# A two-layer attention and mLSTM model on one core: attention output, gates and mixer 1 laid out by channel

## The chip, the core and the metric

The kernel runs on one core of a Trainium2 chip. TensorE (PE), VectorE (DVE), ScalarE (ACT), GpSimd (POOL) and SyncE (SP) each work through their own instructions in order and wait for one another by semaphores. The metric is device time in microseconds, lower is better. "PEld" is TensorE's loading of stationary weights, which overlaps its matmuls.

## The reference, cut to what matters

The input has 2048 latent tokens and 256 context tokens, each 1024 wide, in float32. Layer 1 is a mixer of attention and Fourier mixing, layer 2 a bidirectional mLSTM. Only layer 1 is touched. Its core is:

```python
def attend(q, k, v):                     # 12 query heads, 4 key/value heads, 64 wide
    s = jnp.einsum('bqhgd,bkhd->bhgqk', q, k) * (HEAD_DIM ** -0.5)
    p = jax.nn.softmax(s, axis=-1)
    return jnp.einsum('bhgqk,bkhd->bqhgd', p, v)

def even_mixer(h_lat, h_ctx, w_in, ...):
    q, ga, k, v, u, gb = jnp.split(h @ w_in, EVEN_SPLITS, axis=-1)   # 768,768,256,256,256,256
    ...                                  # norms, rotation of q and k
    y = jnp.concatenate([a * jax.nn.silu(ga), f * jax.nn.silu(gb)], axis=-1)
    return y @ w_out
x = layer_norm(ALPHA * x + g_l * y_lat) * post_ln_gain + post_ln_bias
```

The latent queries attend to all 2304 tokens, the context queries to the 256 of the context. `f` is the Fourier mixing of `u`. "Gates" below means `silu(ga)` and `silu(gb)`, 1024 channels together.

## The kernel before, in words

The program is a chain of stages with a barrier after each: modulation, first projection (`projections`, `pj_`), key heads and context attention (`heads`, `hd_`, with `ContextAttention`, `ca_`), latent attention (`attention`, `al_`), Fourier mixing (`fourier`, `fo_`), mixer 1 (`mixer_out`, `mo_`), second projection (`p_`, `pa_`, `pb_`), the mLSTM scan (`ml_`) and mixer 2 (again `mo_`).

**First projection.** 90 steps: five chunks of 512 columns (`c`), and in each chunk 18 tiles of 128 tokens (`t`). A step is 24 matmuls, in which 128 tokens are the stationary side and 512 weight columns move; each fp32 operand is split in a high and a low part (`split_mm`, L243). ScalarE makes the high part of a tile (L723), VectorE the low part (L855), two steps ahead. Chunks 3 and 4 are the gates; ScalarE evicts them with Silu (L762), SyncE stores them into `s_proj0` (L651). Between the steps, one tile every three steps, the query heads (`QueryHeads`) are loaded back, squared, rotated, transposed and stored. Every engine takes these parts at fixed steps of the same list.

**Latent attention.** 48 blocks of 512 queries of one head, two blocks (p = 0 and 1) to a loop turn. For each block TensorE computes scores twice. The first time (L2346), for the next block, is in 20 tiles with queries on partitions, of which VectorE takes the row maxima (L2269); they rotate over three PSUM slots, so tile x waits for the maximum of tile x - 3. VectorE joins the maxima and negates them (L2275), and SyncE moves them by DMA into the extra row of `qb` (L2158). The second time (L2358, L2359) the keys are on partitions and the row is included, so ScalarE can take the exponential straight away (L2209). The values (L2368) then add up in one PSUM bank: even key tiles in partitions 0 to 63, odd ones in 64 to 127. GpSimd and VectorE add up the exponentials for the denominators (L2235 to L2246, L2283, L2286) into `asum`. ScalarE copies the accumulator to `ot` (L2216), and `folded` (L2380, L2381) adds its two halves with an identity matrix as the moving side and sums `asum` over partitions with a column of ones. The result has tokens on partitions; VectorE takes 4 reciprocals per partition (L2290) and multiplies (L2294), SyncE stores it in `s_attn`, a row per token.

In TensorE's order a block is: values 6 to 8 of the block before, two maxima tiles, scores 0, two maxima tiles, scores 1, and so on, with three values groups in front of scores 3 and 6; `folded` stands between scores 7 and 8.

**Context attention** does the same in small in the heads stage: products with a column of ones beside the values (L1807), a reciprocal of 2 elements per partition (L1812).

**Fourier mixing** ends with 18 result tiles, copied out of PSUM by VectorE (L2587) and stored to `s_four`; the mixer's weights are loaded, split and prepared beside it (L2448, L2452, L2456).

**Mixer 1.** 18 tiles of 128 tokens. Loads of attention, Fourier and gate rows (L2710 to L2712), product (L2839), eight transposes on TensorE (L2884), high part (L2747), low part (L2843), 48 matmuls, then residual, layer norm, gain and store. Transposes of tile n + 1 stand in front of the matmuls of tile n.

## Time and profile before

| what | us |
|---|---|
| median of three runs | 3727.72 (3726.23 to 3730.48) |
| the profiled execution | 3721.77 |
| its span | 3720.1 |
| TensorE matmuls busy | 3435.6 (92%) |
| VectorE busy | 2290.1 (62%) |
| GpSimd busy | 1843.1 (50%) |
| ScalarE busy | 1334.7 (36%) |

Busy time is what an engine's instructions cover; the rest is waiting. The latent attention takes 732 to 1864 us of the span, mixer 1 about 1945 to 2186.

### The profile page before, as it was taken

To read this page: it belongs to the slowest core of one execution; us is meant where nothing else is said; L and a number is where in the kernel's file an instruction comes from. 1 tells how busy PE (TensorE), PEld (TensorE's weight loads), DVE (VectorE), ACT (ScalarE), POOL (GpSimd) and SP (SyncE) were. 2 spreads that over 40 slices of the span, in tenths; PEclk is the share of its full clock that TensorE was granted. 3 is DMA by queue.
4 is the path that set the end of the run, shared out by engine and by line. 5 is a ranking of instruction groups with operands and counts; after the bars stand their busy time and mean duration, and the time that the engine had idled before them with its cause. 6 is when DMAs were issued, how large, how long until landed. Compare 5 with 4: busy or idle time off the path is not lost. (4 is left out here: it accounts for less than half of the span.)

```text
span 3720.1 us, 51212 instructions
## 1 busy us (share of the span) xinstructions
PE 3435.6 (92%) x16884; PEld 2586.8 (70%) x16884; DVE 2290.1 (62%) x3492; ACT 1334.7 (36%) x2240; POOL 1843.1 (50%) x1294
## 2 busy tenths in 40 slices
PE   6999997799999999999959979989999998999798
PEld 4787884456666666666558869877778786887586
DVE  4666642766666666666536654366575645777576
ACT  2432333434444444444320123333443422664200
POOL 1133413657777777777723333433586612444364
PEclk7999997799999999999979989999999999999899
DMA  5234535511111111111065545655545446677563
GB/s 189 99 106 133 142 105 179 189 28 35 34 35 34 37 35 38 35 37 34 17 206 172 189 133 171 206 189 158 175 129 173 142 150 206 214 221 241 198 217 133
DMA packets 357715, 480.18 MB, mean 129 GB/s; under 512 B 83308, under 2 KB 209276, under 8 KB 357392
## 3 DMA queue, kind: packets, MB, share of 16 engines
q1 hardware_dynamic: 291744, 342.18, 29.9%
q10 hardware_dynamic: 54256, 97.73, 8.8%
q0 software_dynamic: 11520, 37.77, 2.6%
q8 instruction: 109, 1.79, 0.2%
q14 instruction: 86, 0.70, 0.1%
HBM read 339.75 MB, written 137.72 MB: 128 GB/s over the span
## 5 line engine op out<-in xcount | busy, mean ns | idle before, releaser
L2269 DVE TENSOR_REDUCE al_mx<-al_sx 128x1 f32<-128x512 f32 (+1 forms) x960 | 562.7, 632 | 267.3 <-PE al_sx L2346 253.7
L2209 ACT ACTIVATE al_e<-al_st 128x1024 f32<-128x1024 f32 x432 | 443.0, 1026 | 579.4 <-PE al_st L2359 569.2
L2239 POOL TENSOR_TENSOR al_acc_p<-al_acc_p,al_e 128x1024 f32<-128x1024 f32 x192 | 456.7, 2379 | 19.8
L245 PE MATMUL pb_acc<-p_whi,pb_r_hi 128*128 128x512 f32 x952 | 378.6, 398 | 39.0 <-DVE pb_r_lo L1616 28.3
L2368 PE MATMUL al_acc<-al_e,vres 128*64 128x512 f32 x1728 | 402.5, 601 | 0.0
L247 PE MATMUL pb_acc<-p_whi,pb_r_lo 128*128 128x512 f32 x952 | 376.3, 395 | 0.0
L246 PE MATMUL pb_acc<-p_wlo,pb_r_hi 128*128 128x512 f32 x952 | 375.5, 394 | 0.0
L1616 DVE TENSOR_TENSOR pb_r_lo<-pb_stg,pb_r_hi 128x512 fp32r<-128x512 f32 x238 | 248.6, 1047 | 165.8 <-ACT pb_r_hi L1514 161.6
L2358 PE MATMUL al_st<-al_qa,kres 128*128 128x512 f32 x864 | 344.7, 399 | 3.6 <-DMA al_qb<-al_negm 3.2
L2359 PE MATMUL al_st<-al_qb,kres 128*128 128x512 f32 x864 | 340.3, 394 | 0.0
L2235 POOL TENSOR_TENSOR al_acc_p<-al_e 128x1024 f32<-128x1024 f32 x48 | 160.3, 3340 | 306.3 <-ACT al_e L2209 306.3
L2346 PE MATMUL al_sx<-kres,al_qx 128*128 128x512 f32 (+1 forms) x960 | 298.1, 393 | 13.3 <-DMA al_qx<-s_q 11.0
L245 PE MATMUL pj_acc<-pj_whi,pj_h_hi 128*128 128x512 f32 x720 | 285.3, 396 | 0.0
L2346 PEld LDWEIGHTS al_sx<-kres,al_qx 128*128 128x128 f32 x960 | 171.9, 191 | 162.2 <-issue 125.8
L247 PE MATMUL pj_acc<-pj_whi,pj_h_lo 128*128 128x512 f32 x720 | 281.8, 391 | 0.0
L246 PE MATMUL pj_acc<-pj_wlo,pj_h_hi 128*128 128x512 f32 x720 | 281.7, 391 | 0.0
L855 DVE TENSOR_TENSOR pj_h_lo<-pj_hall,pj_h_hi 128x1024 fp32r<-128x1024 f32 x90 | 131.0, 1457 | 207.1 <-ACT pj_h_hi L723 207.1
L2368 PEld LDWEIGHTS al_acc<-al_e,vres 128*64 128x64 f32 x1728 | 111.2, 136 | 211.2 <-issue 194.8
L1514 ACT ACTIVATE pb_r_hi<-pb_stg 128x512 fp32r<-128x512 f32 x238 | 149.2, 628 | 270.0 <-PE pb_acc L247 252.6
L245 PEld LDWEIGHTS pb_acc<-p_whi,pb_r_hi 128*128 128x128 f32 x952 | 181.6, 191 | 84.1 <-DVE pb_r_lo L1616 34.2
L245 PE MATMUL mo_acc<-ow_whi,mo_y_hi 128*128 128x512 f32 x544 | 215.6, 396 | 0.0
L247 PE MATMUL mo_acc<-ow_whi,mo_y_lo 128*128 128x512 f32 x544 | 212.8, 391 | 0.0
(320 smaller groups left out, 7287.3 us busy)
## 6 DMA issues: line engine op xcount, KB each, us to landing
pb_stg<-s_hsum ACTq DMA_DIRECT2D x238, 256.0 KB, 2.7
s_proj<-pj_stage SPq DMA_DIRECT2D x90, 256.0 KB, 2.1
s_proj<-pb_out SPq DMA_DIRECT2D x72, 256.0 KB, 3.0
p_wst<-in_w1s ACTq DMA_DIRECT2D x18, 1024.0 KB, 5.9
ml_k<-s_proj SPq DMA_DIRECT2D x36, 512.0 KB, 4.3
ml_v<-s_proj SPq DMA_DIRECT2D x36, 512.0 KB, 8.8
mo_in<-s_proj SPq DMA_DIRECT2D x34, 512.0 KB, 6.3
hm_w<-in_ada_w SPq DMA_DIRECT2D x16, 1024.0 KB, 9.8
```

The source lines that it names most:

```text
L245: nc.tensor.matmul(out, s_hi, m_hi, start=start, stop=False)
L246: nc.tensor.matmul(out, s_hi, m_lo, start=False, stop=False)
L247: return nc.tensor.matmul(out, s_lo, m_hi, start=False, stop=stop)
L1616: V.tensor_tensor(r_lo[:, g % RING], stg[:, g % NSTG], r_hi[:, g % RING].bitcast(F32), ALU.subtract).then_inc(lo_done, 1)
L2209: nc.scalar.activation(e[:, pair(p, j), :, :], st[(NP * p + j) % 2][:, :, 0:W], ACT.Exp).then_inc(e_done, 1)
L2235: nc.gpsimd.tensor_tensor(acc_p[:], e[:, pair(p, 2)], e[:, pair(p, 5)], ALU.add).then_inc(add_p, 1)
L2239: nc.gpsimd.tensor_tensor(acc_p[:], acc_p[:], e[:, pair(p, j)], ALU.add).then_inc(add_p, 1)
L2269: V.tensor_reduce(mx[:, x:x + 1], slots[x % NSX][:, 0:spans[x % NS][1]], AX.X, ALU.max).then_inc(sx_max, 1)
L2346: mm(slots[x % NSX][:, 0:width], qx[:, p, i * P:(i + 1) * P], kres[:, g, lo:lo + width], start=True, stop=True).then_inc(sx_mm, 1)
L2358: mm(dst[:, t, 0:W], kres[:, g, keys], qa[:, p, :], start=True, stop=False)
L2359: y = mm(dst[:, t, 0:W], kres[:, NKV + g, keys], qb[:, p, :], start=False, stop=True)
L2368: y = mm(acc[t * HD:(t + 1) * HD, 0:W], vres[:, 2 * j + t, g, :], e[:, pair(p, j), t, :], start=(j == 0), stop=(j == NP - 1))
```

## The change

**Attention by channel.** The two halves of the accumulator are no longer folded by TensorE. ScalarE copies one half (64 partitions), and VectorE adds the other from PSUM (`joined`): the even block's result goes to `even`, which ScalarE copies to the lower half of `un`, the odd block's to the upper half. TensorE's next values wait for this sum (`un_done`) instead of for ScalarE's copy. Denominators are made for two blocks at once: a 128 x 64 matrix of ones is stationary, `asum` moves, so that the sum stands on 64 partitions. ScalarE copies it out of PSUM, VectorE takes the reciprocal in four pieces of 128 columns between the maxima of the odd block, and one product gives both blocks. The result is stored by channel.

```diff
+            def joined(n, p, v):
+                half, other = slice(p * HD, (p + 1) * HD), slice((1 - p) * HD, (2 - p) * HD)
+                dve.wait_ge(ot_done, n + 1)
+                if p == 0 and not (fixed(n) and n < 2):
+                    dve.wait_ge(kept, v)
+                V.tensor_tensor(even[:] if p == 0 else un[half, :], acc[other, 0:W], ot[half, :], ALU.add).then_inc(un_done, 1)
+            def inverse(v, i):
+                dve.wait_ge(den_out, v + 1)
+                V.reciprocal(rden[:, piece(i)], den[:, piece(i)]).then_inc(rden_done, 1)
+            def norm(v):
...
+                V.tensor_tensor(o[:], un[:], rden[:], ALU.mult).then_inc(o_done, 1)
...
             def body(g, n, p, v, nxt):
+                if started and p == 1:
+                    joined(n - 1, 0, v)
+                elif started:
+                    joined(n - 1, 1, v - 1)
...
                     if j == 7 and nxt is not None:
                         bias(n + 1, 1 - p, v + p)
-                    if j == 8 and started:
-                        norm(n - 1, 1 - p, v - 1 + p)
+                    if paired and j in (1, 2, 4, 5):
+                        inverse(v - 1, (1, 2, 4, 5).index(j))
+                    if paired and j == 7:
+                        norm(v - 1)
```

On TensorE and ScalarE:

```diff
-            def folded(n, p):
...
-                for i in range(nq):
-                    at, cols = i * (HD + 1), slice(i * P, (i + 1) * P)
-                    mm(fo[:, at:at + HD], ot[:, p % 2, cols], fold[:, 0:HD], start=True, stop=True)
-                    y = mm(fo[:, at + HD:at + HD + 1], asum[:, p % 2, cols], ones[:], start=True, stop=True)
-                y.then_inc(fold_mm, 1)
+            def denominators(n, v):
+                pe.wait_ge(asum_done, n + 2)
...
+                for i in range(2):
+                    y = mm(fo[i * HD:(i + 1) * HD, 0:W], ones[:], asum[:, i, :], start=True, stop=True)
+                y.then_inc(den_mm, 1)
...
-                    if j == 7 and started:
-                        folded(n - 1, 1 - p)
+                    if j == 7 and p == 0 and started:
+                        denominators(n - 2, v - 1)
...
+                nc.scalar.activation(ot[half, :], acc[half, 0:W], ACT.Copy).then_inc(ot_done, 1)
+                nc.scalar.activation(den[:], fo[:, 0:W], ACT.Copy).then_inc(den_out, 1)
+                nc.scalar.activation(un[0:HD, :], even[:], ACT.Copy).then_inc(kept, 1)
```

The context attention does likewise: 64 values columns, then 64 columns of ones, stationary; a reciprocal of 256 columns for every two heads.

**Gates by channel.** In chunks 3 and 4 the weights are stationary and up to four token tiles (512 tokens) move. A group of four tiles is four steps: the first two do the first half of the 1024 inputs, the last two the second half, so the four results of a group appear in its last two steps; five PSUM banks rotate. The result goes to a new `s_gt`, a row per channel. The query heads load into two buffers instead of three.

```diff
+    turned_q = [c >= GATED if L0 else C1_Q <= c * CH < C1_Q + D for c, _ in steps]
+    base = [k - t % 4 if turned_q[k] else k for k, (_, t) in enumerate(steps)]
...
+    ahead = [min(K - 1, base[k] + (5 if tiles[k] == 4 and k > base[k] else 3) if turned_q[k] else k + (1 if c == 0 else 2)) for k, (c, _) in enumerate(steps)]
...
+            def turned_products(k, c):
...
+                if n == 4:
+                    pe.wait_ge(lo_done, first + (2 if step < 2 else 4))
+                    half, columns = step // 2, range(step % 2 * 2, step % 2 * 2 + 2)
+                    part = range(half * KP, half * KP + KP)
...
+                        mm = split_mm(nc, dst, whi[:, c % 2, i, at:at + P], wlo[:, c % 2, i, at:at + P], moving(h_hi, k, i), moving(h_lo, k, i), i == 0, i == KD - 1)
```

**Fourier and mixer 1.** The last Fourier matmuls swap their sides, and their result stays in SBUF (`four`) by channel: no `s_four`, no stores. Mixer 1 loads attention and gates by channel (rows of 128 tokens, 512 B) and does the product in two parts, straight in the layout that the matmuls need; its transposes go, and the product of tile n + 2 moves in front of the normalisation. Loads of a tile now wait for the low part two tiles before.

```diff
-                    sp.dma_start(ins[:, p, 0, 0:QW], s["attn"][rows, :]).then_inc(in_ld[p], 16)
-                    sp.dma_start(ins[:, p, 0, QW:D], s["four"][rows, :]).then_inc(in_ld[p], 16)
-                    sp.dma_start(ins[:, p, 1, :], s["proj0"][rows, C_GATE:W0_COLS]).then_inc(in_ld[p], 16)
+                    sp.dma_start(ins[:, p, 0, 0:QW].rearrange("p (k n) -> p k n", n=P), s["attn"][:, rows].rearrange("(k p) n -> p k n", p=P)).then_inc(in_ld[p], 16)
+                    sp.dma_start(ins[:, p, 1, :].rearrange("p (k n) -> p k n", n=P), s["gt"][:, rows].rearrange("(k p) n -> p k n", p=P)).then_inc(in_ld[p], 16)
...
             def turned(n, p, v):
+                if L0:
+                    return
```

## Rows read from the trace of the kernel before

**Rows 1.** Busy time by stretch: start:end, length, then PE, PEld, DVE, ACT, POOL, clock.
```profile
400.00:603.00 203.00, 201.30 (x912) 166.57 (x910) 89.76 (x81) 69.76 (x89) 43.99 (x23) 1.00 0.38 107
603.00:732.00 129.00, 82.02 (x424) 43.81 (x424) 78.32 (x209) 64.48 (x351) 93.79 (x125) 0.72 0.76 241
732.00:1864.00 1132.00, 1116.52 (x5184) 684.22 (x5184) 757.17 (x1200) 471.82 (x480) 792.52 (x336) 0.99 0.13 34
1945.00:2186.00 241.00, 216.34 (x1016) 180.45 (x1014) 154.33 (x196) 26.95 (x31) 82.27 (x76) 0.95 0.49 170
```

**Rows 2.** Timeline of TensorE, one attention block: start, duration, engine, line, tiles, count.
```profile
1000.65 2.80 PE L2368 MATMUL al_acc<-al_e,vres 128*64 128x512 f32 x12
1003.37 0.73 PE L2346 MATMUL al_sx<-kres,al_qx 128*128 128x512 f32 x2
1003.94 0.39 PE L2358 MATMUL al_st<-al_qa,kres 128*128 128x512 f32 x1
...
1004.87 0.62 PE L2346 MATMUL al_sx<-kres,al_qx 128*128 128x512 f32 x2
...
1020.88 0.33 PE L2380 MATMUL al_sx<-al_fold,al_ot 128*128 128x64 f32 x2
...
1022.58 0.49 PE L2358 MATMUL al_st<-al_qa,kres 128*128 128x512 f32 x1
...
1023.70 2.79 PE L2368 MATMUL al_acc<-al_e,vres 128*64 128x512 f32 x12
```

**Rows 3.** Timeline of VectorE in the same block; idle time before and its releaser in brackets.
```profile
1003.91 3.66 DVE L2269 TENSOR_REDUCE al_mx<-al_sx 128x1 f32<-128x512 f32 x6 [3.56 <-PE al_sx L2346]
...
1009.32 2.33 DVE L2283 TENSOR_TENSOR al_acc_d<-al_e 128x1024 f32<-128x1024 f32 x1
...
1016.20 1.22 DVE L2286 TENSOR_TENSOR al_acc_d<-al_acc_d,al_e 128x1024 f32<-128x1024 f32 x1
...
1021.10 0.17 DVE L2275 TENSOR_REDUCE al_negm<-al_mx 128x4 fp32r<-128x20 f32 x1
```

**Rows 4.** Timelines of ScalarE and GpSimd in the same block.
```profile
1003.49 0.60 ACT L2216 ACTIVATE al_ot<-al_acc 128x512 f32<-128x512 f32 x1 [1.71 <-PE al_acc L2368]
...
1009.29 1.27 POOL L2246 TENSOR_TENSOR al_asum<-al_acc_p 128x512 f32<-128x512 f32 x1
1016.25 3.41 POOL L2235 TENSOR_TENSOR al_acc_p<-al_e 128x1024 f32<-128x1024 f32 x1 [5.68 <-ACT al_e L2209]
```

**Rows 5.** VectorE's groups by form: count, then busy us, mean ns of one.
```profile
L1635 DVE TENSOR_TENSOR pb_out<-pb_acc,pb_s 128x512 f32<-128x512 f32 x34 | 23.4, 689 | 36.5 <-PE pb_acc L247 36.5
L3087 DVE RECIPROCAL ml_den<-ml_den 128x1 f32<-128x1 f32 x128 | 21.0, 164 | 4.4
L2290 DVE RECIPROCAL al_rden<-al_sx 128x4 f32<-128x4 f32 x48 | 8.8, 183 | 85.8 <-PE al_sx L2381 85.8
```

**Rows 6.** Negated maxima (durations, first and last start) and the first scores.
```profile
L2275 DVE TENSOR_REDUCE al_negm<-al_mx x48: 173/174/175, 744.5 to 1826.2; 128x4 fp32r<-128x20 f32 x48
...
748.70 0.77 PE L2358 MATMUL al_st<-al_qa,kres 128*128 128x512 f32 x1 [3.24 <-DMA al_qb<-al_negm]
```

**Rows 7.** Timeline of mixer 1: its start, and one tile change.
```profile
1937.89 1.23 DVE L2839 TENSOR_TENSOR mo_y<-mo_in 128x1024 f32<-128x1024 f32 x1 [12.03 <-DMA mo_in<-s_proj]
...
1946.27 0.78 PE L245 MATMUL mo_acc<-ow_whi,mo_y_hi 128*128 128x512 f32 x1
...
2005.18 1.03 PE L2884 MATMUL mo_tp<-keep_ident,mo_y 128*128 128x128 f32 x8
...
2005.97 0.48 PE L245 MATMUL mo_acc<-ow_whi,mo_y_hi 128*128 128x512 f32 x1
```

**Rows 8.** DMA issues: count, KB each, median us from issue to landing.
```profile
ml_qt<-s_qt SPq DMA_DIRECT2D x32, 512.0 KB, 6.2
```

**Rows 9.** Timeline at the end of the Fourier stage.
```profile
1929.42 2.34 POOL L2456 TENSOR_TENSOR ow_wlo<-ow_wst,ow_whi 128x1024 fp32r<-128x1024 f32 x1 [1.38 <-ACT ow_whi L2452]
```

**Rows 10.** Waits, 180 to 603 us: total us, times, longest.
```profile
ACT hq_hi L306 <- DMA s_q<-hq_lo: 145.5, 17, 14.5
```

More of the change, by code:

```diff
@@ L607, in projections, with source, slot, moving @@
     w1_st = hall[:, 0:KP, NT - 4:, :].rearrange("p k t n -> p k (t n)")
+    def source(k):
+        n, t = tiles[k], steps[base[k]][1]
+        part = slice((k - base[k]) * KD // n, (k - base[k] + 1) * KD // n)
+        return hall[:, part, t:t + n, :]
+    def slot(h, k):
+        return h[:, k % RING].rearrange("p (k t) n -> p k t n", t=tiles[k])
+    def moving(h, k, i):
+        per = KD // tiles[k]
+        return slot(h, base[k] + i // per)[:, i % per]
     def evicted(eng, k):
@@ L2180, in body @@
                     row(n + 1, 1 - p)
-                if not (fixed(n) and n == 0):
-                    store(n - 1, prev_p(p, 1))
+                if p == 1 and not (fixed(n) and n < 2):
+                    store(n - 3, v - 1)
                 if more:
@@ L2188, in _ @@
             over_blocks(sp, body)
[L2189 to L2191 removed]
+            store(TOTAL - 2, TOTAL // 2 - 1)
+            sp.wait_ge(stored, 16 * TOTAL)
         @block.scalar
@@ L2330, in _ @@
             over_blocks(dve, body)
-            norm(TOTAL - 1, TOTAL - 1, (TOTAL - 1) // 2)
+            joined(TOTAL - 1, 1, TOTAL // 2 - 1)
+            for i in range(NPIECE):
+                inverse(TOTAL // 2 - 1, i)
+            norm(TOTAL // 2 - 1)
         @block.tensor
@@ L2498, in _ @@
                 out_weights.load(sp, k)
[L2499 to L2508 removed]
+            for k in range(2, KD):
+                out_weights.load(sp, k)
         @block.gpsimd
```

334 lines of the change are left out of this document (181 added, 153 removed).

## The prediction

> **What bounds the kernel now.** I read the stages first. TensorE's matmul side is busy 1116.5 of 1132.0 us in the latent attention, 216.3 of 241.0 in mixer 1 and 201.3 of 203.0 in the gate chunks of the first projection; only the heads stage leaves it idle (82.0 of 129.0) [rows 1]. So in three of the four stages that the change touches, an instruction taken from TensorE is worth its time, unless its gap is filled by a wait. Then the timeline of one attention block, because 48 of them make the stage. The stretch from 1000.65 to 1023.70, values to values, is one block: 23.05 us [rows 2]. In it VectorE has 0.36 to 3.6 us of idle time in four places, about 6.6 us in all [rows 3]: it is not the bound, but it stands one step behind TensorE, since a score tile for the maxima may be overwritten only when the maximum three before it is done.
>
> **Attention, what goes.** Per block, eight fold and eight denominator matmuls: first at 1020.88, next scores at 1022.58, 1.70 us, and those scores start 0.33 us apart in place of 0.23, so 1.80 us [rows 2]. What comes: per two blocks two fp32 matmuls of 64 columns by 512, four passes. The values have that form: twelve passes from 1000.65 to 1003.37, 0.227 each [rows 2], so 0.91 and about 0.2 for the switches: 1.1 us. The other bounds for it are nothing and the fold's own 1.8. If nothing else were late, a pair of blocks went from 46.10 to 46.10 - 3.60 + 1.10 = 43.60 us: 2.5 us for each of 24 pairs, 60 us. That is the most that this part can give.
>
> **What is late next.** Three new things sit on VectorE, which must feed the maxima.
> 1. The joined sum (accumulator half plus ScalarE's copy) is the first instruction of a block in VectorE's order. It waits for ScalarE's copy, 0.60 us from 1003.49 [rows 4], and costs 0.69 like the 512-column operations from PSUM [rows 5]. Counted from the block's start (1000.65): copy 2.84 to 3.44, joined 3.48, first maximum 4.08 in place of 3.26 [rows 3]. Its result is there at 4.81; TensorE wants the slot for the fourth score tile at 4.45 (the pair at 1004.87 [rows 2], second 0.23 later). A slip of 0.36 us in every block. What queues behind joined is all of VectorE's block; who waits is TensorE. Values of the next block need the accumulator at 7.4, joined is done at 4.2: no loss there. ScalarE's two extra copies per pair (0.6 us each) run while TensorE does values, where ScalarE idles 1.71 us before its copy [rows 4].
> 2. The reciprocal now has 128 columns in each of four pieces. The trace has it with 1 and 4 elements: 164 and 183 ns [rows 5], so 6.3 ns an element and 183 + 124 x 6.3 = 0.97 us a piece, 3.9 us a pair, all in the odd block. The low end is 0.18 (a fixed cost only), the high end 46 ns an element (183 by 4), which the 1-element row speaks against; I take 0.97, since only the two rows together say how it grows. In the odd block, after the fourth maximum, piece 0 runs 6.48 to 7.38, so the fifth maximum comes at 7.84 instead of before 7.45: slip 0.39. Piece 1 pushes the first addition from 8.67 to 10.6; there it no longer meets GpSimd's sum and takes 1.2 instead of 2.3 us [rows 3, 4], which gives 1.1 back. Piece 2 delays the thirteenth maximum to 15.51, wanted at 15.17: slip 0.34. Piece 3 puts the second addition at 17.8 (it was at 15.55), in the middle of a GpSimd addition; I let it wait to 18.55, which costs 0.15 more at the last score tile. Sum of slips in the odd block: 0.36 + 0.39 + 0.34 + 0.15 = 1.24.
> 3. The row of negated maxima goes by DMA to the next block's first scores. At the start of the stage that path stands free: negation at 744.5, scores at 748.70, waiting for the DMA: 4.2 us [rows 6]. In steady state they are 5.9 us apart (1021.10 to 1003.94 + 23.05 = 1026.99), so 1.7 us of slack and the fold is 1.8 of it. In the odd block the row lands 0.25 us late; in the even block the 1.1 us of denominators cover it.
>
> Even block: 23.05 - 1.80 + 1.10 + 0.36 = 22.7; odd: 23.05 - 1.80 + 1.24 + 0.25 = 22.7. Pair 45.4 against 46.1: 0.7 x 24 = 17 us gained of the possible 60. The end of the stage has no cover: denominators, ScalarE's copy, four reciprocals, product and store stand in a row. Fold, reciprocal and product took about 4.2 us after the last sum; now 1.7 (matmuls at the low clock) + 0.65 + 3.9 + 0.7 = 7.0: **+2.7 us**. Bounds of the whole attention part: -57 (all hidden) to +40 (third rival).
>
> The Trainium skill, VectorE: DVE Perf Modes, "First, the fixed hardware budget", says that Reciprocal is an iterative divide with a repeat count of 8. At the page's 0.96 GHz this would be 8.3 ns an element, an estimate of 1.2 us a piece, where the two rows say 6.3 ns. By the page the odd block would lose some 0.6 us more, attention gain only 3 us, and the total come out near 3715.
>
> **Heads stage.** Context attention: reciprocal of 256 columns per two heads, 183 + 252 x 6.3 = 1.77 us, six times, for twelve of 2 elements (under 0.18, by the rows of 1 and 4 [rows 5]); products and matmuls come out even. +8.6 us of VectorE work in a stage where it is busy 78.3 of 129.0 [rows 1]; the last pair stands at the end of the stage and costs 1.6 us openly. Bounds 1.6 and 8.6; I take **+3**.
>
> **Gate chunks.** Weights stand and 512 tokens move: 24 matmuls of 512 columns a step as before, the same conversions and the same 256 KB stores. Nothing to gain where TensorE is busy 99% [rows 1]. But results of a group of four steps come only in its last two, so ScalarE, which evicts in order, stands up to 2.5 steps behind, and with it SyncE's stores and the query heads' loads and stores queued behind them on SyncE. ScalarE already waits 8.6 us on average for the store of the query heads, 17 times [rows 10], and TensorE hides it with five steps of lead. One case of scaled queries behind two conversions held until the middle of the third step costs half a step (2.7 us), three more about 0.5: **+4**, bounds 0 and +25 (half a step in each of nine groups).
>
> **Fourier mixing.** The same matmuls with operands swapped, the same evictions into SBUF. The eighteen stores go and the weights' loads move past them on SyncE, but the stage ends with GpSimd's low part of the last weights at 1929.42 + 2.34 = 1931.76 [rows 9]; that chain (load, ScalarE, GpSimd, two buffers) is untouched. **0**; up to 2 us of gain.
>
> **Mixer 1.** Eight transposes per tile: 2005.18 to 2005.97 and 0.1 us for the slower start after them, 0.89 us [rows 7], for 17 tiles in the steady part: **-15**. The period falls from 11.5 to 10.6 us. VectorE does 8.6 us a tile there (154.3 by 18 [rows 1]), so it doesn't take over. The start: gate product at 1937.89, first product of the mixer at 1946.27, with two transposed tiles and conversions between [rows 7]. Now product 1.4, high part 1.0, low part 1.2: 1941.6. The load in front may be slower for its shorter rows; I allow 0.7: **-4**. The loads get rows of 512 B: the queries of the scan, 512 KB in such rows, land in 6.2 us [rows 8]. Attention and gates together are 896 KB: 10.8 us if all of the 6.2 grows with the bytes, 6.2 if none does; I take 9, since small transfers have a fixed part too. They may start when the low part two tiles earlier is done, one period (10.6 us) before they are wanted, so they fit, narrowly.
>
> **Sum.** -17 + 2.7 + 3 + 4 + 0 - 15 - 4 = -26 us. The profiled execution took 3721.8 us (span 3720.1), 6 us under the median of 3727.7; durations hardly differ, so I take the difference off the median: 3701.
>
> **Rivals.**
> - All of VectorE's work finds room (shorter reciprocals, or maxima with more slack than I read): attention gains 57. For it: 6.6 us of idle in each block [rows 3] against 2.4 us of added work a block (2 x 0.69 + 3.9 + 0.69 less two old reciprocals and products, about 1.2, by 2). Against: the idle stands after TensorE's values, not where the pieces are. 3727.7 - 57 + 3 + 4 - 19 = 3659.
> - The gates' and attention's loads bind mixer 1, and its 15 us are lost: 3716. For it the 6.2 us row; against it a DMA share of 0.49 in the stage [rows 1].
> - The gate chunks starve TensorE for half a step per group, +25 instead of +4: 3722.
> - The other side: VectorE becomes the bound in the odd blocks through the port that it shares with GpSimd. An addition that starts beside one of GpSimd's takes 2.33 us instead of 1.22, as at 1009.32 against 1016.20, and at 1016.25 it is GpSimd that waits (3.41 instead of 2.4) [rows 3, 4]. Pieces move the second addition behind GpSimd's first; if GpSimd's chain, 2.4 us each with 0.1 between, keeps the port for one more, the maxima and the negation come 2.4 us later and TensorE waits for all of it: odd block 25.1, pair 47.8, 24 x 1.7 = +41 in place of -17: 3760. It decides from a wait above 0.7 us + what the sum has (pair above 46.1). The Trainium skill, SBUF - State Buffer, "SBUF: two separate sides", calls this port pair an exclusive lock held for the whole instruction by whichever starts first, for VectorE operations with two SBUF inputs; the trace agrees with it (2.33 against 1.22), and by it only the additions and the last product can be hit, not maxima, reciprocals or joined sums.
>
> **Chances.** My forecast 0.50; all hidden 0.22; loads bind mixer 1 0.08; gate chunks 0.07; port 0.13. A measurement of this kernel can tell 0.2%, 7.5 us, from no change. Faster: the first three, 0.80; same: the fourth, 0.07; slower: 0.13. Own range of the forecast 3685 to 3718; the range for 8 in 10 reaches to the hidden case and past the fourth: 3655 to 3735.
>
> **What would show it.** Attention period of 45.4 us a pair; reciprocals of about 0.97 us; TensorE waiting at the fourth score tile for VectorE's maximum, 0.3 to 0.4 us a block; even blocks without a wait for the row, odd ones with a short one. Mixer 1 with a period near 10.6 us and its first product about 4 us earlier after the stage's start. Gate chunks with TensorE idle of a few us. It would be wrong if the pair were at 43.6 (then the slips are none) or over 46.1, or if the second additions took over 2.4 us, or if mixer 1 waited for its loads.

## The result, and the profile after

The changed kernel takes 3763.9 us (median of 4 runs, 3760.6 to 3768.1), the kernel before 3727.0 in the same comparison. The ratio is 1.0105, 95% interval 1.0091 to 1.0119: slower by 39 us (37 between the two medians) where 26 us less were forecast. The profiled execution took 3761.6 us, its span is 3759.9. The stages from both traces, by the starts of the instructions named (us). One trace has a scatter of its own: in the eleven traces with the changed kernel's gate chunks these take 217.9 to 222.1 us, and in the ten with its heads stage that takes 147.7 to 153.6.

| from ... to | before | after | change | forecast |
|---|---|---|---|---|
| start to the projection's last product | 600.9 | 622.8 | +21.9 | +4 |
| to the first latent score tile (heads stage) | 131.6 | 150.8 | +19.2 | +3 |
| to the last latent scores | 1115.8 | 1122.8 | +7.0 | -17 |
| to the Fourier stage's first load | 17.1 | 22.6 | +5.6 | +2.7 |
| to mixer 1's first product | 80.9 | 74.6 | -6.3 | -4 |
| to mixer 1's last product | 211.0 | 198.6 | -12.5 | -15 |
| to the end | 1562.8 | 1567.8 | +5.0 | 0 |

The busy time by stretch (start:end, length, then PE, PEld, DVE, ACT, POOL, granted clock, DMA share, GB/s) of the changed kernel: gate chunks, heads, latent attention, mixer 1's products. In the gate chunks TensorE was never idle between two products; now it is for 11.2 us, and for 0.5 more at the head of the stretch shown. The attention loses 18 us of TensorE's work and still gets longer.

```profile
404.00:623.00 219.00, 207.36 (x1008) 174.15 (x1008) 85.69 (x81) 67.23 (x86) 40.19 (x23) 0.98 0.34 97
623.00:773.00 150.00, 96.03 (x425) 45.13 (x424) 85.13 (x197) 65.20 (x352) 87.87 (x119) 0.77 0.66 207
773.00:1919.00 1146.00, 1098.86 (x4512) 591.68 (x4512) 868.81 (x1272) 496.55 (x528) 799.46 (x336) 0.98 0.13 33
1993.00:2192.00 199.00, 198.48 (x863) 164.10 (x864) 145.05 (x195) 19.88 (x18) 85.78 (x69) 0.98 0.57 188
```

**Gate chunks.** The timeline of the changed kernel around its longest gap, SyncE, ScalarE, VectorE, GpSimd, TensorE, and the busy time behind two gaps. SyncE stands for 7.42 us at the stores of results that are not finished (488.26); the query heads' stores queued behind them land late, so ScalarE can overwrite the high part only at 501.63. ScalarE itself stands for 4.59 us at such a result (494.73), so the weights' high part comes late, GpSimd's low part of it (497.27), and behind that the query heads' scale `hq_rs` (503.11). VectorE's conversions take 6.01 us beside GpSimd's (2.36 alone), then VectorE waits 1.28 us for that scale (506.34). The query heads' low part comes at 507.22, and TensorE, whose transposes need it, has waited 5.47 us. So the last waits of this gap end on GpSimd and VectorE, and not on ScalarE's high part.

```profile
488.26 7.42 SPq L674 DMA_DIRECT2D s_gt<-pj_stage  x2
...
494.73 0.60 ACT L788 ACTIVATE pj_stage<-pj_acc 128x512 f32<-128x512 f32 x1 [4.59 <-PE pj_acc L247]
...
501.63 0.81 ACT L310 ACTIVATE hq_hi<-pj_tp 128x768 fp32r<-128x768 f32 x1 [2.62 <-DMA s_q<-hq_lo]
...
498.11 6.01 DVE L881 TENSOR_TENSOR pj_h_lo<-pj_hall,pj_h_hi 128x1024 fp32r<-128x1024 f32 x2 [3.82 <-ACT pj_h_hi L749]
...
506.34 0.96 DVE L361 TENSOR_TENSOR hq_turn<-hq_turn,hq_rs 128x768 f32<-128x768 f32 x1 [1.28 <-POOL hq_rs L334]
507.22 0.95 DVE L367 TENSOR_TENSOR hq_lo<-pj_tp,hq_hi 128x768 fp32r<-128x768 f32 x1
...
497.27 4.62 POOL L823 TENSOR_TENSOR pj_wlo<-pj_wst,pj_whi 128x2048 fp32r<-128x2048 f32 x1 [9.85 <-ACT pj_whi L733]
...
503.11 3.13 POOL L334 TENSOR_TENSOR hq_rs<-hq_rs,hq_power 128x12 f32<-128x12 f32 x1
...
508.32 1.51 PE L375 MATMUL pj_tp<-keep_ident,hq_turn 128*128 128x128 f32 x6 [5.47 <-DVE hq_lo L367]
...
451.00:476.00 25.00, 24.79 (x115) 20.51 (x116) 10.23 (x12) 9.77 (x12) 9.32 (x5) 1.00 0.45 133
508.00:533.00 25.00, 24.68 (x154) 22.86 (x155) 13.01 (x13) 7.39 (x10) 8.21 (x5) 0.93 0.33 91
```

**Heads.** One pair of tiles of the changed kernel. The pairs repeat every 14.8 us (reciprocals at 690.33, 705.20, 720.02), where two tiles took about 10 before. TensorE waits 2.73 us for the turned keys and then runs its values at about half the rate (3.55 us for eight; 1.94 at the full clock). VectorE's 1.76 and 0.42 us stand between values and the next turned keys.

```profile
694.45 0.65 PE L2108 MATMUL hd_tk<-keep_ident,hd_rot 128*128 128x128 f32 x4 [2.73 <-DVE hd_rot L2060]
...
695.51 3.55 PE L1855 MATMUL ca_res<-ca_e,ca_v 128*64 128x256 f32 x8
...
703.22 1.94 PE L1855 MATMUL ca_res<-ca_e,ca_v 128*64 128x256 f32 x8
...
705.20 1.76 DVE L1863 RECIPROCAL ca_rden<-ca_res 128x256 f32<-128x256 f32 x1 [0.72 <-PE ca_res L1855]
706.99 0.42 DVE L1865 TENSOR_TENSOR ca_o<-ca_res,ca_rden 128x256 f32<-128x256 f32 x1
...
708.58 0.69 DVE L2060 TENSOR_TENSOR hd_rot<-hd_turn,hd_rs 128x512 f32<-128x512 f32 x1
```

**Latent attention.** The 48 negations give the period: first and last start, 47 blocks apart, so the mean pair is (1876.1 - 785.5) / 23.5 = 46.41 us; before it was 46.03 [rows 6]. "Mean pair" below is always that.

```profile
L2349 DVE TENSOR_REDUCE al_negm<-al_mx x48: 173/174/176, 785.5 to 1876.1; 128x4 fp32r<-128x20 f32 x48
```

TensorE, ScalarE, VectorE and GpSimd in the even block from 1019.29 to 1042.81 and, for the second addition, in the odd one behind it. The fourth score tile starts at 1024.57, 0.71 us after the third where it was 0.23 [rows 2]. The first addition (1029.00) waits 0.18 us for GpSimd's combining sum, then takes 2.32 us beside GpSimd's last sum. The product takes 2.61 us beside GpSimd's chain, and 2.6 or more in 16 of the 24 of the run (0.69 in the others). ScalarE's copy of the even result waits 1.32 us for it (1021.82), and the accumulator's copy stands behind (1022.48). In the odd block the second addition takes 2.10 us beside GpSimd's first sum (22 of the 24 take over 2 us), where it took 1.22 before [rows 3]. The reciprocal shown is of the odd block before.

```profile
1024.57 0.50 PE L2435 MATMUL al_sx<-kres,al_qx 128*128 128x512 f32 x1 [0.32 <-DVE al_mx L2343]
...
1040.66 1.08 PE L2467 MATMUL al_sx<-al_asum,al_ones 128*64 128x512 f32 x4
...
1021.82 0.63 ACT L2284 ACTIVATE al_un<-al_even 64x512 f32<-64x512 f32 x1 [1.32 <-DVE al_o L2382]
1022.48 0.59 ACT L2270 ACTIVATE al_ot<-al_acc 64x512 f32<-64x512 f32 x1
...
1003.11 0.94 DVE L2373 RECIPROCAL al_rden<-al_den 128x128 f32<-128x128 f32 x1
...
1019.12 2.61 DVE L2382 TENSOR_TENSOR al_o<-al_un,al_rden 128x512 f32<-128x512 f32 x1 [0.22 <-issue]
1023.11 0.68 DVE L2368 TENSOR_TENSOR al_un<-al_acc,al_ot 64x512 f32<-64x512 f32 x1 [1.38 <-ACT al_ot L2270]
...
1029.00 2.32 DVE L2357 TENSOR_TENSOR al_acc_d<-al_e 128x1024 f32<-128x1024 f32 x1 [0.18 <-POOL al_acc_p L2316]
...
1060.57 2.10 DVE L2360 TENSOR_TENSOR al_acc_d<-al_acc_d,al_e 128x1024 f32<-128x1024 f32 x1
...
1026.51 2.39 POOL L2316 TENSOR_TENSOR al_acc_p<-al_acc_p,al_acc_d 128x1024 f32<-128x1024 f32 x1
1028.98 1.27 POOL L2320 TENSOR_TENSOR al_asum<-al_acc_p 128x512 f32<-128x512 f32 x1
...
1059.23 2.36 POOL L2309 TENSOR_TENSOR al_acc_p<-al_e 128x1024 f32<-128x1024 f32 x1 [5.91 <-ACT al_e L2262]
```

**End of the attention.** The last values start at 1896.62 (1848.60 before); GpSimd's last sum ends 12.2 us later (9.9 before), and from there denominators, copy, four reciprocals, product and store take 10.1 us (6.8 before).

```profile
1907.54 1.26 POOL L2320 TENSOR_TENSOR al_asum<-al_acc_p 128x512 f32<-128x512 f32 x1
1908.86 1.97 PE L2467 MATMUL al_sx<-al_asum,al_ones 128*64 128x512 f32 x4 [9.44 <-POOL al_asum L2320]
1910.88 0.60 ACT L2277 ACTIVATE al_den<-al_sx 128x512 f32<-128x512 f32 x1 [10.82 <-PE al_sx L2467]
1911.51 3.39 DVE L2373 RECIPROCAL al_rden<-al_den 128x128 f32<-128x128 f32 x4 [10.74 <-ACT al_den L2277]
```

**Mixer 1** starts with the gate product at 1989.82 and the first product 3.7 us later, 8.4 before [rows 7].

```profile
1989.82 0.96 DVE L2916 TENSOR_TENSOR mo_in<-mo_in 128x768 f32<-128x768 f32 x1 [9.85 <-DMA mo_in<-s_gt]
...
1993.52 0.79 PE L245 MATMUL mo_acc<-ow_whi,mo_y_hi 128*128 128x512 f32 x1 [14.17 <-DVE mo_y_lo L2931]
```

### The profile page after: what moved, and what is told of

The parts are those of the page before. It is cut to its first block and busy times, and to the rows that moved or that the text cites. A ratio compares the mean times of both kernels' runs of the same rounds, so it can differ in the third digit from the quotient of the medians.

```text
span 3759.9 us, 49801 instructions
## 1 busy us (share of the span) xinstructions
PE 3423.0 (91%) x16164; PEld 2492.1 (66%) x16164; DVE 2411.2 (64%) x3570; ACT 1361.3 (36%) x2288; POOL 1849.0 (49%) x1288
## 5 line engine op out<-in xcount | busy, mean ns | idle before, releaser
L2343 DVE TENSOR_REDUCE al_mx<-al_sx 128x1 f32<-128x512 f32 (+1 forms) x960 | 549.0, 625 | 63.4 <-PE al_sx L2435 58.9
L2313 POOL TENSOR_TENSOR al_acc_p<-al_acc_p,al_e 128x1024 f32<-128x1024 f32 x192 | 484.9, 2526 | 20.0 <-POOL al_acc_p L2313 0.4
L2435 PE MATMUL al_sx<-kres,al_qx 128*128 128x512 f32 (+1 forms) x960 | 331.4, 408 | 35.0 <-DVE al_mx L2343 21.8
L2309 POOL TENSOR_TENSOR al_acc_p<-al_e 128x1024 f32<-128x1024 f32 x48 | 139.0, 2896 | 308.2 <-ACT al_e L2262 308.2
L245 PE MATMUL mo_acc<-ow_whi,mo_y_hi 128*128 128x512 f32 x544 | 215.1, 395 | 14.2 <-DVE mo_y_lo L2931 14.2
L246 PE MATMUL mo_acc<-ow_wlo,mo_y_hi 128*128 128x512 f32 x544 | 213.5, 393 | 0.0
L2447 PEld LDWEIGHTS al_st<-al_qa,kres 128*128 128x128 f32 x864 | 163.0, 189 | 70.1 <-issue 36.9
L247 PEld LDWEIGHTS pb_acc<-p_whi,pb_r_lo 128*128 128x128 f32 x952 | 181.4, 191 | 40.3
```

The costliest lines, as they stand in the source:

```text
L245: nc.tensor.matmul(out, s_hi, m_hi, start=start, stop=False)
L246: nc.tensor.matmul(out, s_hi, m_lo, start=False, stop=False)
L247: return nc.tensor.matmul(out, s_lo, m_hi, start=False, stop=stop)
L2313: nc.gpsimd.tensor_tensor(acc_p[:], acc_p[:], e[:, pair(p, j)], ALU.add).then_inc(add_p, 1)
L2343: V.tensor_reduce(mx[:, x:x + 1], slots[x % NSX][:, 0:spans[x % NS][1]], AX.X, ALU.max).then_inc(sx_max, 1)
L2435: mm(slots[x % NSX][:, 0:width], qx[:, p, i * P:(i + 1) * P], kres[:, g, lo:lo + width], start=True, stop=True).then_inc(sx_mm, 1)
```

## The experiments

Ratios are to the kernel before, on the same chip; the changed kernel has 1.0105. "Gates" is first gate product to last product of the projection, "heads" to the first latent score tile, "end" from the last latent scores to the Fourier stage's first load, all in us. e2, e4 and e7 leave work of the reference out; they only measure.

| run | ratio, 95% interval | what moved |
|---|---|---|
| e1 | 1.0068 (1.0051 to 1.0085) | gates 218.3 to 204.1 |
| e2 | 1.0050 (1.0033 to 1.0067) | heads 150.8 to 136.8 |
| e3 | 1.0118 (1.0101 to 1.0135) | mean pair 46.54 |
| e4 | 1.0078 (1.0061 to 1.0095) | mean pair 46.23, end 4.0 shorter |
| e5 | 1.0166 (1.0145 to 1.0188) | mean pair 47.2 |
| e6 | 1.0148 (1.0128 to 1.0168) | mean pair 47.0 |
| e7 | 1.0057 (1.0040 to 1.0073) | mean pair 45.76, end 5.2 shorter |
| e8 | 1.0092 (1.0064 to 1.0121) | heads 139.9 |
| e9 | 1.0092 (1.0075 to 1.0110) | mean pair 46.14 |
| e10 | 1.0023 (1.0013 to 1.0032) | gates 204.1, heads 136.7 |
| e11 | 1.0144 (1.0126 to 1.0163) | mean pair 46.88 |
| e12 (before) | 0.9995 (0.9982 to 1.0007) | mean pair 45.92 |
| e13 | 0.9996 (0.9987 to 1.0005) | mean pair 45.92 |
| e14 | 0.9995 (0.9986 to 1.0004) | mean pair 45.84 |
| e15 | 1.0097 (1.0082 to 1.0113) | mean pair 45.93 |
| e16 | 0.9967 (0.9954 to 0.9980) | mean pair 45.55 |
| e17 | **0.9923 (0.9909 to 0.9936)** | mean pair 44.78 |
| e18 (before) | 0.9994 (0.9984 to 1.0004) | mean pair 45.89 |

### e1: the order in the gate chunks

```diff
+    ended = [[base[k] + 2 * (k - base[k]) - 4 + i for i in range(2)] if tiles[k] == 4 and k > base[k] + 1
+             else [] if tiles[k] == 4 else [k] for k in range(K)]
-    ahead: base[k] + (5 if tiles[k] == 4 and k > base[k] else 3)
+    ahead: base[k] + (5 if tiles[k] == 4 and k > base[k] + 1 else 3)
 (scalar, sync, step k)
-    evict k; store k
+    for u in ended[k]: evict u; store u
```

> The changed kernel with another order in the gate chunks alone: ScalarE's evictions and SyncE's stores of a group of four steps stand in the order at the third and fourth step, where the results are finished, and the conversions for the next group one step later. No work is added or taken away. Theory: what the gate chunks lose (404.5 to 622.5 in the changed kernel, 218 us against 197) is TensorE waiting for the query heads' low part, which waits for ScalarE and SyncE standing behind evictions of unfinished results; 13.8 us of idle time and about 5 of the lower clock after it. Then the stretch falls to 199 to 205 us and the total to about 3747 (3743 to 3752). Rival: the form itself costs it (192 matmuls of 256 columns at 0.120 us instead of half of 0.221, banks, conversions for four tiles at once): the stretch stays above 212 and the total above 3757.

Gates 204.1 us, total -14: the theory holds. No gap is left in TensorE's row after the first product; one of 2.3 us is left ahead of it. The edit moves the evictions, the stores and two of the conversions together, so it shows that their order costs the 14 us, not how they share them.

```profile
406.00:610.00 204.00, 203.78 (x1005) 172.91 (x1006) 86.58 (x81) 66.84 (x85) 40.69 (x23) 0.99 0.37 105
```

### e2, e8, e10: the heads stage

```diff
 e2: -reciprocal(rden[:], res[:, W:2 * W])    +reciprocal(rden[:, 0:4], res[:, W:W + 4])
 e8: scaled(n); bias(n - 3)
+    norm(n - 7)
     normal(n); low_part(n - 1)
-    norm(n - 6)
 e10: e1 + e8, and on TensorE
-    scores(n - 5); values(n - 6); mod.products(n)
+    scores(n - 5); mod.products(n); values(n - 6)
```

> The changed kernel with the context attention's six reciprocals over 4 columns instead of 256 (the rest of the buffer holds ones, so the context's denominators are left out). Theory: the reciprocal stands on the path of each pair of tiles, transposes, values, reciprocal, product, turned keys, next transposes: 6 x 1.58 = 9.5 us of the stage's loss of 19.4 go (stage 150.6 to about 141), total 3754; the rest belongs to the values matmuls, 8 of 256 columns (1.94 us) where there were 8 of 65 (1.00). Rival 1: the reciprocal explains all of it, since its wait also drops the clock: stage 131 to 134, total 3745. Rival 2: it is hidden and the matmuls' form is all: stage 148 or more.

> The changed kernel with the context attention's reciprocal and product one tile later in VectorE's order, behind the next turned keys instead of ahead of them (and the store one tile later); nothing is left out. Theory: it is the order that puts 2.2 us between values and TensorE's next transposes, and TensorE's wait (2.73 us a pair) that drops its clock to 0.5 (3.55 us for eight values matmuls that take 1.94): the stage falls from 150.6 to 138 to 143, total about 3753. Rival: the values of the next even head wait for the product now, and the pair stays near 14.8 us: stage above 148, total above 3761.

> The changed kernel with the new order in the gate chunks (first experiment), the context's reciprocal and product one tile later (eighth), and the context's values on TensorE behind the modulation's products instead of ahead of them. Theory: the two stages' losses are independent and both are matters of order: gate chunks 204 us, heads stage at most 140 (lower if the values now find their denominators' product done, 132 to 138), total 3763 - 14 - 12 = 3737. Rival: what one stage gives comes back in the next (the heads stage was 2.8 us longer when the gate chunks were shorter): total above 3746.

e2 gives back 14.0 us (11 to 17 with the scatter of the stage), more than the 9.5 us of reciprocals in it: rival 1 was nearer, since the wait costs clock as well. TensorE's busy time for the same matmuls falls from 96.03 us (in 150) to 91.96. e8 leaves nothing out and gives 10.9; its total is unclear by itself (the interval reaches from -15 to +6 us against the changed kernel's 1.0105). e10 is clear: 31 us less than the changed kernel in all, heads 136.7. The reciprocal need not be shorter, it must not stand ahead of the next turned keys. The heads stages of e2, e8 and e10:

```profile
627.00:764.00 137.00, 91.96 (x429) 43.60 (x428) 76.04 (x198) 65.28 (x352) 89.64 (x119) 0.79 0.73 228
```

```profile
632.00:772.00 140.00, 92.83 (x426) 42.89 (x426) 87.07 (x197) 65.05 (x352) 90.21 (x119) 0.77 0.69 223
```

```profile
615.00:751.00 136.00, 91.80 (x424) 41.08 (x424) 87.04 (x197) 64.94 (x352) 89.92 (x119) 0.78 0.72 229
```

### e3 to e6: single moves on VectorE, and the reciprocals taken away

```diff
 e3: (vector, block) joined(n - 1) ahead of the first maximum -> behind the fourth
 e4: -V.reciprocal(rden[:, piece(i)], den[:, piece(i)])
     +V.reciprocal(rden[:, i * P:i * P + 4], den[:, i * P:i * P + 4])
 e5: add(n, p, 0) behind the eighth maximum -> behind the tenth
 e6: e3 + e5
```

> The changed kernel with the joined sum behind the fourth maximum of a block instead of ahead of the first, on VectorE alone. Theory: the joined sum at the head of the block makes TensorE wait at the fourth score tile, 0.58 and 0.60 us more than in the kernel before in the two blocks of a pair. With it behind, that wait is gone: pair of blocks 46.3 to about 45.2, attention 1145 to about 1118, total about 3737. Rival: VectorE is short of time in the whole first part of the block, and the wait only moves to the sixth or eighth tile: pair 46.0 or more, total above 3756.

> The changed kernel with each of the latent attention's four reciprocal pieces over 4 columns instead of 128 (the rest holds ones: most denominators are left out). Theory: 4 x 0.76 us go from VectorE in every second block, and with them the slips of 0.30 and 0.45 us at the eighth and the fourteenth to sixteenth score tile and about 0.15 elsewhere; the pair goes from 46.3 to 45.4, the end of the stage is 3.1 us shorter, total about 3739. Rival: the product beside GpSimd's additions (2.61 us where it takes 0.69 alone) is what delays the block, and the reciprocals are not: pair 46.1 or more, total above 3755.

> The changed kernel with VectorE's first addition of a block behind the tenth maximum instead of the eighth; nothing else. Theory (GpSimd's chain): that addition overwrites what GpSimd's combining sum reads, and runs beside GpSimd's last sum (2.33 us where it takes 1.22 alone); two maxima later GpSimd stands idle, 1.1 us of VectorE come back in each block that had it, and the slips at the tenth to sixteenth score tile (0.09 to 0.45 us) shrink: attention 1145 to about 1132, total about 3750. Rival: the addition filled the 2.7 us in which TensorE does values and VectorE has no tile; moved, it stands before tiles that are wanted, attention 1150 or more, total above 3765.

> The addition later as above, and the joined sum behind the fourth maximum. Theory (GpSimd's chain): with the joined sum late alone the slip at the fourth tile went (1.06 to 0.46 us) and came back at the tenth (0.58 to 1.00) and the eighth (0.84 to 1.61), where the addition waited 0.48 us for GpSimd's combining sum. With both moved no addition meets GpSimd: pair 46.3 to about 45.0, total about 3732. Rival (VectorE has no room at all): each shift only moves the slip, pair 46.2 or more, total above 3760.

All four theories fell; in e4 the rival did too by its total (3752, where it had over 3755). In e3 the fourth tile is on time (third and fourth tile 0.45 us together, 1.04 in the changed kernel), and the lost time comes back at the twelfth tile (its pair takes 1.00 for 0.58; the expectations call it the tenth) and the eighth (1.61 for 0.84): the first addition, now later, waits for GpSimd:

```profile
1033.84 2.33 DVE L2357 TENSOR_TENSOR al_acc_d<-al_e 128x1024 f32<-128x1024 f32 x1 [0.48 <-POOL al_acc_p L2316]
```

In e4 3.0 us of VectorE's work are gone from each pair, and the mean pair falls by 0.18 us only: the slips at the eighth and sixteenth tile are gone, but the first addition waits 1.11 us for the same sum, and the twelfth tile comes 0.94 later. So neither the joined sums nor the reciprocals are the loss by themselves. e5 takes the addition out of TensorE's values, where it stood free: its rival was right.

### e7, e9, e11, e12: GpSimd's chain and the fold

```diff
 e7: -tensor_tensor(acc_p[:], acc_p[:], e[:, pair(p, j)], ALU.add)
     +tensor_tensor(acc_p[:, 0, :], acc_p[:, 0, :], e[:, pair(p, j), 0, :], ALU.add)
 e9: (tensor, even block, ahead of values 0 to 2; ScalarE copies fo to un once a pair)
     +for i in range(2):
     +    mm(fo[i * HD:(i + 1) * HD, 0:W], fold[:], ot[:, i, :], start=True, stop=True)
     -V.tensor_tensor(even or un[half, :], acc[other, 0:W], ot[half, :], ALU.add)
 e11, e12: -IN_POOL = (2, 5, 4, 6, 7, 8)    +IN_POOL = (2, 4, 5, 6, 7, 8)
```

> The changed kernel with GpSimd's four chained additions over half of their columns (512 instead of 1024; half of these sums is left out, and the denominators get 1 added). Theory: the attention's period is a loop, late score tiles, late exponentials, GpSimd's chain (about 17 us of a block of 23.15) later by about 1 us than before the change, VectorE's first addition waiting for it, late maxima. With the chain 5 us shorter the addition waits for nothing: pair 46.3 to 45.0 or less, and the end of the stage 5 us shorter: total 3763 to about 3728. Rival: VectorE's own added work (joined sums, reciprocals, product) is the whole loss: pair 46.0 or more, only the end of the stage gains, total about 3756.

> The changed kernel with the two halves of the accumulator joined on TensorE again, once per pair of blocks, by channel (two matmuls of 64 columns by 512, as the denominators, ahead of the even block's first values; ScalarE copies both halves per block and the joined result once per pair). VectorE's two joined sums (0.69 us each) go. Theory: the joined sum is what makes the fourth score tile late; its slip of 0.6 us goes in both blocks, TensorE has 1.1 us more work a pair, and the first additions meet GpSimd's end as before: pair 46.3 to 45.9 to 46.2, total 3753 to 3762, with the fourth tile at 0.46 us in both blocks. Rival: the slip moves behind, as it did when the joined sum was only put later, and TensorE's 1.1 us come on top: pair above 47, total above 3785.

> The changed kernel with GpSimd's first sum of a latent block over the third and fifth exponentials instead of the third and sixth, so that its chain can start one step (1.4 us) earlier; the same five sums. Theory (GpSimd's chain sets when VectorE's first addition may run, and how late the end of the stage is): the chain ends 1.0 to 1.4 us earlier, the first addition takes 1.22 us instead of 2.33, attention falls by 10 to 24 us, total 3740 to 3753. Rival: the start now meets VectorE's second addition (1.22 us, 2.17 in one block of the pair already), which waits 2.4 us for it ahead of the last score tiles: pair above 46.5, total above 3768.

> The kernel before with the same earlier start of GpSimd's sums. If GpSimd's chain also sets the pace of the kernel before, it gains as the changed one does. Theory: there VectorE has room (6.6 us of idle a block), its additions' waits cost TensorE nothing, and only the end of the stage gets 1.4 us shorter: 3722 to 3727. Rival: it gains as much as the changed kernel, then the order is a reserve of both and no part of the explanation: below 3715.

e7 is the largest step of one edit to the changed kernel: 0.65 us a pair, though VectorE's work is all there. Both additions of the even block now take 1.2 us and most products 0.94. It is half of what the theory asked for. Its negations:

```profile
L2349 DVE TENSOR_REDUCE al_negm<-al_mx x48: 173/174/177, 788.6 to 1864.0; 128x4 fp32r<-128x20 f32 x48
```

e9: the fourth tile is on time in both blocks, as expected, and the pair pays about 1.0 us of TensorE for it. e11's rival was right: the second addition takes up to 3.37 us in odd blocks and 2.15 to 2.28 in even ones (mostly 2.18 and 1.22 in the changed kernel). e12: in the kernel before the second additions lengthen too (mostly 2.15 to 2.28 us, 1.22 without the edit), and its time stays the same.

### e13 to e18: place, and the combining sum

```diff
 e13: e10 + e9; (vector, odd block) pieces 0, 1 ahead of the first maximum, 2, 3 at j = 4, 5
 e14: as e13, but pieces 2, 3 and the product ahead of the next even block's first maximum
 e15, e16, e17, e18: the changed kernel, e13, e14, the kernel before, each with
      for i, j in enumerate(IN_POOL[2:]):
+         if i == 2:
+             gpsimd.tensor_tensor(acc_p[:], acc_p[:], acc_d[:], ALU.add).then_inc(comb_done, 1)
          gpsimd.tensor_tensor(acc_p[:], acc_p[:], e[:, pair(p, j)], ALU.add)
-     gpsimd.tensor_tensor(acc_p[:], acc_p[:], acc_d[:], ALU.add).then_inc(comb_done, 1)
```

> The tenth kernel (gate chunks and context in the new order) with the fold by channel of the ninth, and the first two reciprocals of a pair ahead of the odd block's first maximum instead of behind the fourth and the sixth. There VectorE is idle: negation at 1040.78, denominators copied at 1044.43, first maximum at about 1046 in the changed kernel. Theory (place, not sum): two of four reciprocals become free, the slip at the eighth tile (0.16 to 0.30 us) goes, the block reaches its first addition earlier: mean pair from 46.14 to 45.8 or less, total 3731.9 - 7 - 8 = 3717 (3712 to 3722). Rival (the sum counts, VectorE has no free time that TensorE does not pay): mean pair 46.1 or more, total 3724 or more.

> As the thirteenth, and the other two reciprocals and the product at the head of the next even block, ahead of its first maximum (3.3 us of idle time between the negation and the first score tile); the store follows there. Theory: the odd block loses all its slips from reciprocals (0.3 and 0.45 us), the even block pays up to 1 us where the product runs beside GpSimd's chain (1.1 to 2.6 us instead of 0.69): mean pair 45.4 to 45.7, total 3707 to 3715. Rival: the product, locked behind GpSimd's sums, makes the first four maxima late in every even block: mean pair above 46.2, total above 3727.

> The changed kernel with GpSimd's combining sum (of VectorE's part) ahead of its last two additions instead of behind them; the same work. VectorE's first addition of the next block then finds its buffer free some 5 us earlier. Theory (the semaphore): the addition goes between two of GpSimd's instructions and takes 1.2 us instead of 0.2 + 2.3, mean pair from 46.41 to 45.9 or less, total 3752 or less. Rival (the port): it waits as long for the instruction that GpSimd then has under way, mean pair 46.3 to 46.6, total 3759 to 3770.

> The thirteenth kernel with the combining sum sooner. Theory (the semaphore): mean pair from 45.92 to 45.4 or less, total 3709 or less against 3721 before. Rival (the port): 45.8 or more, total 3718 or more.

> The fourteenth kernel with the combining sum sooner. Its even blocks' first addition waited 2.38 us for the combining sum and then ran 2.33 beside GpSimd's last sum; the odd ones 0.67 and 2.32. Theory (the semaphore): mean pair from 45.84 to 45.0 or less, total 3700 or less. Rival (the port): 45.7 or more, total 3716 or more.

> The kernel before with the combining sum ahead of GpSimd's last two additions. Theory: there VectorE's wait behind GpSimd costs TensorE nothing (its score tiles start 0.44 to 0.57 us apart throughout), so the mean pair stays at 46.0 and the total within 5 us of 3721. Rival: it gains as e17 did over e14, a us a pair: total below 3705.

e13 and e14 bring the change level with the kernel before. Both mean pairs, 45.92 and 45.84, lie between theory and rival, and e14's trace says why: in the even block shown nothing on VectorE is late but the first addition, which stands 2.38 us for GpSimd's combining sum (1.65 in the middle one of the 24) and then 1.1 us beside the last one; the twelfth tile comes 1.4 us late.

```profile
1044.71 2.33 DVE L2362 TENSOR_TENSOR al_acc_d<-al_e 128x1024 f32<-128x1024 f32 x1 [2.38 <-POOL al_acc_p L2321]
...
1042.25 2.36 POOL L2321 TENSOR_TENSOR al_acc_p<-al_acc_p,al_acc_d 128x1024 f32<-128x1024 f32 x1
1044.69 1.28 POOL L2325 TENSOR_TENSOR al_asum<-al_acc_p 128x512 f32<-128x512 f32 x1
```

e15, e16 and e17 take that semaphore's wait away. e16 falls by 0.37 us a pair (its theory asked for 0.5) and ends 12 us below the kernel before. e17 falls by 1.06 us a pair to 44.78 and is the fastest version, 29 us below the kernel before. e15 falls by 0.48 a pair, 11 us over the stage in its trace, but its total moved by 3 us only (1.0097 against 1.0105, intervals that overlap); what it is worth alone is not settled. The port that VectorE shares with GpSimd is still there: e17's first addition takes 3.39 us in the even block shown (2.8 to 3.4 in nearly all), beside GpSimd's instruction, but wait and addition together took 4.71 in the block of e14 above, and TensorE no longer notices. e17's even block, its attention stage and its negations:

```profile
1035.80 3.39 DVE L2364 TENSOR_TENSOR al_acc_d<-al_e 128x1024 f32<-128x1024 f32 x1
...
746.00:1851.00 1105.00, 1085.50 (x4608) 603.66 (x4608) 852.88 (x1224) 498.16 (x528) 841.08 (x336) 0.98 0.14 34
...
L2356 DVE TENSOR_REDUCE al_negm<-al_mx x48: 173/174/176, 758.0 to 1810.3; 128x4 fp32r<-128x20 f32 x48
```

e18 is the control: the same step in the kernel before shortens most of its first additions (over 2 us in 17 of 48, before in 47) and its total stays the same. The wait was a loss of the change, not a reserve of both.

## Why the prediction was wrong, step by step

**"Gate chunks: +4, bounds 0 and +25."** It was +21.9, and the mechanism was the rival's, "the gate chunks starve TensorE for half a step per group" (chance 0.07). I had read that results come only in a group's last two steps and that SyncE, ScalarE and the query heads queue behind them, and then priced one case of it. Four gaps for the query heads' low part come to 10.2 us, the longest (5.47) a whole step and not half a one, and a gap can cost clock as well: granted 0.93 in the 25 us behind the longest, 0.92 in the 21 us with one of 2.7 us ahead of the first product, but 1.00 behind the one of 3.14 us that ends at 451.2. e1 shows that order alone is 14 us of it. Of the rest, 192 matmuls of 256 columns at 0.120 us, where half of 0.227 was counted, are 1.3 us, and the gap ahead of the first product, which e1 keeps, is 2.3.

**"Heads: +3, bounds 1.6 and 8.6. Products and matmuls come out even."** It was +19.2, outside the bounds. The duration was right (1.76 us; forecast 1.77). Wrong was to look for cover in idle shares: the reciprocal stands in VectorE's order ahead of the next tile's turned keys, so it is on the path once per pair (e8: 10.9 us by order alone), the wait lowers TensorE's clock (e2 gives 14.0 for 9.5), and the values are not even: 8 matmuls of 256 columns take 1.94 us, 8 of 65 took about 1.0. Over the twelve groups of eight that is 11 us more of TensorE's time; no run shows how much of it the stage pays.

**"Pair of blocks 45.4 against 46.1."** It was 46.41 against 46.03. Fold, denominators (1.01, forecast 1.1), reciprocal (0.94 for 0.97) and joined sum (0.69) were sized rightly, and the odd block came out as forecast, 22.7 (1042.81 to 1065.50), with the first addition short there (1.27 us at 1053.13, 1.22 in most) as said. The even block took 23.5 for 22.7 (means over the run: even 23.7, odd 22.6): the slip at the fourth tile is 0.58 to 0.60 us, not 0.36; the late row of negated maxima costs 0.34 there, where 0.25 was put in the odd block. One part was a copy called free: in even blocks ScalarE's copy of the even result waits for the product that GpSimd holds up, and the accumulator's copy behind it starts 3.19 us after the block (1022.48) instead of 2.84 [rows 4]. In the same block of e7, where the product takes 0.93 us, it is 2.84 again, and the stretch from these values to the next is 8.09 us instead of 8.36. What failed beyond these sizes is the kind of sum: each slip was priced by itself. TensorE's slips make the exponentials late, these GpSimd's chain (its combining sum starts 7.2 us after the even block does, 6.2 before), and that VectorE's first addition of the even block, which delays score tiles again. So single reliefs were mostly taken back there (e3, e4, e9). With pieces and product at the heads of the blocks and the wait behind GpSimd gone the pair reached 44.78 (e17), near the forecast's "if nothing else were late" (43.6) with e9's fold of about 1.0.

**The end of the stage**, +2.7 forecast: it was +5.6. Its own chain took 3.3 more, by the reciprocals as said (e4 takes 3.0 off this chain), and GpSimd's lateness 2.3, which the step had not.

**Fourier and mixer 1**: -19 forecast, -18.8 measured. From gate product to first product the start gained 4.7 us (8.4 to 3.7). A tile takes 10.88 us where it took 11.79 (the forecast had 10.6 and 11.5): 0.91 less, as forecast, but for 15 tiles and not 17, and the first takes 1.3 more, since TensorE comes from a wait of 14.2 us and has a granted clock of 0.84 in its first 20 us (0.95 before). That makes 12.5 for 15. The near sum of the two is luck: the start's 6.3 for 4 covers it.

**The rivals.** All hidden (0.22) fell with the attention. The loads did not bind mixer 1: TensorE is busy 198.48 of 199.0 us there. The port rival's total, 3760, is near the result by accident: it had +41 us in the attention, and attention gave +12.6. Its mechanism is there in small: at its own place, the second addition of the odd block, 2.1 to 2.2 us instead of 1.22 (the forecast had let it wait 0.75 there), and at the product, but no instruction was held for a whole sum more. The Trainium skill, SBUF - State Buffer, "SBUF: two separate sides", has VectorE operations with two SBUF inputs and GpSimd's exclude each other for a whole instruction; the trace agrees: product 0.69 to 2.87 us, first addition 1.22 or 2.3 (up to 3.39 in e17), while all 48 joined sums, with one input in PSUM, took 0.68 to 0.69. On the reciprocal the rows were right: 0.94 us for 128 columns and 1.76 for 256 are 6.4 ns an element. The estimate of 8.3 ns, made from the repeat count of 8 (the Trainium skill, VectorE: DVE Perf Modes, "First, the fixed hardware budget"), was too dear.

**What stays open**: some 4 us up to the end of the gate chunks and 2 to 5 of the heads stage that no order tried gave back (for the latter the 11 us of longer values are an untested candidate), how the 14 us of e1 divide between evictions, stores and conversions, and the 5 us behind mixer 1, of which 1.7 lie at its end and the rest in stages whose code did not change.

## What to carry to other kernels

An operation put into an in-order stream is priced by what stands behind it, not by the engine's idle share: for each, name the next instruction on its engine that TensorE waits for, and the cover ends there. Where results of a group of steps finish together, put their evictions and stores in the order at the step where they finish; queued at their nominal step they hold everything behind them on that engine and queue. Where three engines form a loop, look at all its waits together: relieving one alone mostly moved the slip (e3, e4, e9), and a run that removes work (e4, e7) tells which wait takes over.

## What the runs showed of the hardware

- A short wait of TensorE can cost more than itself: after 2.73 us of idle time eight matmuls of 256 columns took 3.55 us instead of 1.94, most of it at the lower of the clock's two levels (1.2 GHz); taking 9.5 us of VectorE's work out of such waits gave 14.0. Not each wait did: behind one of 3.14 us in the gate chunks the granted clock stayed 1.00.
- Matmuls of 128 by 128 weights with 256 moving columns follow each other every 0.120 us, with 512 every 0.227: splitting costs 6%.
- VectorE's addition of 128 x 1024 with two SBUF inputs takes 1.22 us alone and 2.1 to 3.4 beside GpSimd's additions; GpSimd waits in turn (3.41 us instead of 2.36).
